# Moving the conditioning product from TensorE to VectorE, shortening a mixing round from ten J turns to eight, and loading exponential's table earlier

## The reference, cut to what matters

```python
b_c, c_c, h_c, q, k, v, g_conv, g_attn = split(xn @ w_in)
y_conv = b_c * causal_dwconv(c_c * h_c, conv_w_mix)
z = q @ k.T * scale                       # for each of 16 heads
log_fail = where(causal, log_sigmoid(z) - z, 0)
a = exp(log_sigmoid(z) + sums of log_fail over the keys between)
o = a @ v
merged = sigmoid(g_conv + b0) * (y_conv @ w_proj_conv) + sigmoid(g_attn + b1) * (o @ w_proj_attn)
mix = merged @ w_out
```

## Time and profile before

| | |
|---|---|
| time, median of 3 runs | 1852.38 us (1851.7 to 1852.97) |
| the profiled execution's own time | 1852.97 us |
| its span | 1851.2 us |
| PE busy | 1757.1 us (95%) |
| DVE, ACT, POOL busy | 1023.7, 897.6, 359.6 us |
| mixing stage (the eight rounds) | about 53 to 506 us of the span |
| gates; stage of `w_out` | about 506 to 678 us; 678 to 735 us |
| granted clock of PE, mean | 0.98 |
| a round in the middle of the mixing stage | 55.1 us |
| weights of a job (512 KB), median from issue to landing | 3.6 us |

### The profile page before, as it was taken

The page is one execution under the profiler, slowest core; times in us unless marked ns, Lnnn a source line. Parts: engine busy times, 40 slices in busy tenths (PEclk is TensorE's granted clock), DMA queues, the critical chain, the costliest instruction groups (busy, mean ns, idle before and its releaser), DMA issues.

```text
span 1851.2 us, 30779 instructions
## 1 busy us (share of the span) xinstructions
PE 1757.1 (95%) x11685; PEld 1574.6 (85%) x11685; DVE 1023.7 (55%) x1538; ACT 897.6 (48%) x1213; POOL 359.6 (19%) x520
## 2 busy tenths in 40 slices
PE   5899999999999999999999999999999999999996
PEld 5899999999999998899998888778877777788885
DVE  3455665655633336787565234477577777754443
ACT  3576666666633334333333222367565565633332
POOL 0011101111100003498880784000000000000001
PEclk9999999999999999799999997999999999999998
DMA  3222223222222235244333443665221221233332
GB/s 119 69 68 81 75 72 91 79 65 72 81 80 91 91 124 185 49 145 133 100 130 101 137 135 104 238 171 169 74 74 52 80 74 51 79 103 121 123 97 102
DMA packets 68034, 189.11 MB, mean 102 GB/s; under 512 B 15284, under 2 KB 19572, under 8 KB 67832
## 3 DMA queue, kind: packets, MB, share of 16 engines
q1 hardware_dynamic: 64040, 176.04, 30.2%
q0 software_dynamic: 3920, 12.06, 2.4%
HBM read 165.76 MB, written 19.95 MB: 100 GB/s over the span
## 4 chain that ended last, share of the span: by engine, by line
PE 70%; DVE 9%; ACT 9%; issue 6%; DMA 3%; POOL 1%; SPq 1%; ACTq 0%; DVEq 0%
PE J L870 25%; PE J L1139 17%; PE J L886 7%; PE J L1108 6%; DMA WR<-weights 3%; PE Z L926 2%; PE J L1274 2%; PE J L1264 2%; PE J L1319 2%; DVE WL L1874 2%; POOL E L2520 1%; DVE MX L2396 1%; ACT E L1477 1%; ACT E L1473 1%; PE Z L948 1%
## 5 line engine op out<-in xcount | busy, mean ns | idle before, releaser
L1874 DVE TENSOR_TENSOR WL<-WR,WH 128x1024 fp32r<-128x1024 f32 x271 | 356.3, 1316 | 310.8 <-ACT WH L1403 302.6
L1403 ACT ACTIVATE WH<-WR 128x1024 fp32r<-128x1024 f32 x271 | 285.3, 1054 | 241.7 <-DMA WR<-weights 118.6
L870 PE MATMUL J<-XH,WH 128*128 128x258 f32 (+1 forms) x1376 | 285.6, 289 | 30.8 <-issue 11.0
L870 PE MATMUL J<-XH,WL 128*128 128x258 f32 (+1 forms) x1376 | 281.8, 287 | 0.0
L870 PE MATMUL J<-XL,WH 128*128 128x258 f32 (+1 forms) x1376 | 275.7, 285 | 0.0
L870 PEld LDWEIGHTS J<-XH,WH 128*128 128x128 f32 x1376 | 219.6, 193 | 37.6 <-issue 26.3
L870 PEld LDWEIGHTS J<-XH,WL 128*128 128x128 f32 x1376 | 217.2, 193 | 0.0
L870 PEld LDWEIGHTS J<-XL,WH 128*128 128x128 f32 x1376 | 213.9, 191 | 0.1
L2520 POOL TENSOR_SCALAR_AFFINE_SELECT E<-E 128x128 f32<-128x128 f32 (+2 forms) x160 | 52.2, 364 | 449.3 <-DVE E L1953 239.1
L2538 POOL TENSOR_TENSOR SA<-SQ 128x512 f32<-128x512 f32 (+1 forms) x3 | 3.9, 1314 | 682.0 <-ACT SQ L1659 492.4
L1139 PE MATMUL J<-X2H,WH 128*128 128x512 f32 x168 | 68.8, 410 | 1.7 <-ACT X2H L1671 1.7
(11 more groups left out here) (432 smaller groups left out, 4162.9 us busy)
## 6 DMA issues: line engine op xcount, KB each, us to landing
WR<-weights SPq DMA_DIRECT2D x271, 512.0 KB, 3.6
CPS<-cp_dram SPq DMA_DIRECT2D x8, 576.0 KB, 6.0
cp_dram<-CQR POOLq DMA_DIRECT2D x16, 144.0 KB, 2.8
cp_dram<-CQI POOLq DMA_DIRECT2D x16, 144.0 KB, 2.8
X<-tokens SPq DMA_DIRECT2D x4, 528.0 KB, 5.3
H<-tokens SPq DMA_DIRECT2D x8, 264.0 KB, 3.8
bp_dram<-BQR POOLq DMA_DIRECT2D x8, 256.0 KB, 2.3
bp_dram<-BQI POOLq DMA_DIRECT2D x8, 256.0 KB, 3.1
```

Source lines behind the costliest of these rows:

```text
L870: mm = pe.matmul(o[:, 512 * h:512 * h + half], ws[:, s, w], xs[:, a:a + half], start=(k == 0 and i == 0 and part != WITH_LOW), stop=(k == ...
L1403: act.activation(WH[:, n % SPLIT, :], WR[:, n % RAW, :], ACT.Copy).then_inc(w_hi, 1)
L1874: dve.tensor_tensor(WL[:, n % SPLIT, :], WR[:, n % RAW, :], WH[:, n % SPLIT, :].bitcast(F32), ALU.subtract).then_inc(w_lo, 1)
```

## The change

The 24 `ada` jobs leave the stream of jobs. Their raw weights are loaded by SP into two buffers of their own, `AW`, three for each round of `gates`, and DVE multiplies them by the numbers of `c` and sums them (`modulation`), behind `ML` of each round of `gates`: two loads of four instructions of 256 columns and one of two instructions of 512 columns in a round, each waiting for the one before. In the stage of `w_out`, behind the second job, PE sums the partitions with 24 matmuls of one column (`sum_mod`), and DVE makes `MB` and `GG` behind the seventh. The way over DRAM, `turn_mod`, `CHL` and their copies go. ACT waits for the last `modulation` ahead of the first square of that stage.

The turned values go to `ZT` (four transposes) and a corner of job c_c's own `J` bank (`VTAIL`, one matmul), so that they take no turn; the empty turn goes as well. A round has eight turns, and job v now waits for the reading of q, no longer of k. PE waits for `v_lo` ahead of job b_c. A round has 6 weight jobs for 8. DVE does `head_out(h)` ahead of `YL`. Behind the logarithm of each `softplus` (and `head_out`), ACT runs an exponential of one column (`load_exp`). The loop's body holds two rounds for one, with the first two and the last two written out; DVE's `gates` is written out in full.

```diff
+            def load_ada(i):
+                if i >= 2:
+                    sp.wait_ge(ada_done, i - 1)
+                row = ROW_OUT + 2 * (i // 3) + 1 if i % 3 == 2 else ROW_MIX + 8 * (i // 3) + 6 + i % 3
+                sp.dma_start(AW[i % 2][:], weights[row]).then_inc(ada_landed[i % 2], 16)
+            for m in range(DT - 1):
+                load_weights(N_GATE + 4 * m + 4, ROW_GATE - N_GATE)
+                load_weights(N_GATE + 4 * m + 6, ROW_GATE - N_GATE)
+                if m == 0:
+                    sp.wait_ge(pv_done, HEADS)
+                for i in range(3 * m, 3 * m + 3):
+                    load_ada(i)
...
+            load_one(N_OUT)
+            load_one(N_OUT + 1)
+            for m in range(DT):
+                load_one(N_OUT + 2 + m)
                 if m == 0:
+                    for i in range(3 * DT - 3, 3 * DT):
+                        load_ada(i)
                     sp.wait_ge(job_done, N_OUT)
...
+            def sum_mod():
+                pe.wait_ge(ada_done, 3 * DT)
+                for b in range(24):
+                    src = MACC[:, P * b:P * (b + 1)] if b < 16 else MLAST[(b - 16) // 4][:, P * (b % 4):P * (b % 4 + 1)]
+                    mm = pe.matmul(ZT[:, b:b + 1], src, ONES[:, 0:1], start=b == 0, stop=True, skip_group_check=True)
+                mm.then_inc(mod_summed, 1)
...
             def turn_values(t):
-                pe.wait_ge(read_out[slot(t)], nth(t))
-                for kt in range(5):
-                    w = min(P, L1 - kt * P)
-                    mm = pe.transpose(J[t % 2][0:w, P * kt:P * (kt + 1)], VT[:, kt * P:kt * P + w], IDENT[:])
-                mm.then_inc(vt_done, 1)
+                for kt in range(4):
+                    pe.transpose(ZT[:, P * kt:P * (kt + 1)], VT[:, kt * P:(kt + 1) * P], IDENT[:])
+                pe.matmul(VTAIL[t % 2], VT[:, 4 * P:L1], IDENT[:],
+                          start=False, stop=True, skip_group_check=True).then_inc(vt_done, 1)
...
             def mix(m, last=False):                      # PE
-                n, t, h = N_MIX + 2 + 8 * m, T_MIX + 10 * m, 2 * m
-                job(n, t + 4, XH, XL)
+                n, t, h = N_MIX + 2 + 6 * m, T_MIX + 8 * m, 2 * m
+                job(n, t + 3, XH, XL)
                 pe.wait_ge(read_out[slot(t + 1)], nth(t + 1) + 1)
                 pe.wait_ge(read_out[slot(t + 2)], nth(t + 2) + 1)
                 scores(h)
                 if m.base or m.reg is not None:
-                    values(h - 1, t + 5)
-                job(n + 1, t + 6, XH, XL, start=LIVE, half=HALFK)
-                turn_values(t + 7)
-                ada(n + 2, 2 * P, True, False, m)
-                ada(n + 3, 2 * P, False, True, m)
-                job(n + 4, t + 8, XH, XL, start=LIVE, half=HALFK)
+                    values(h - 1, t + 4)
+                job(n + 1, t + 5, XH, XL, start=LIVE, half=HALFK)
+                turn_values(t + 5)
+                job(n + 2, t + 6, XH, XL, start=LIVE, half=HALFK)
                 accumulate(h)
-                job(n + 5, t + 9, XH, XL, start=LIVE, half=HALFK)
+                pe.wait_ge(v_lo, val(m + 1))
+                job(n + 3, t + 7, XH, XL, start=LIVE, half=HALFK)
                 scores(h + 1)
-                pe.wait_ge(read_out[slot(t + 7)], nth(t + 7) + 1)
-                values(h, t + 10)
...
+            def load_exp():                              # ACT
+                act.activation(EXP1[:], ONES[:, 0:1], ACT.Exp)
...
                 split_hi(n + 4)
                 softplus(h)
                 if later:
-                    head_out(h - 1, m - 1, t + 5)
+                    head_out(h - 1, m - 1, t + 4)
+                load_exp()
                 fail_hi(h)
...
-                split_hi(n + 6)
-                split_hi(n + 7)
-                split_hi(n + 8)
+                split_hi(n + 6)
                 weight_exp(h)
                 weight_hi(h)
-                split_hi(n + 9)
...
                 if not last:
-                    q_hi(m + 1, t + 11, n + 6)
-                    split_hi(n + 10)
-                    k_hi_(t + 12, n + 7)
+                    q_hi(m + 1, t + 9, n + 4)
+                split_hi(n + 7)
+                if not last:
+                    split_hi(n + 8)
+                    k_hi_(t + 10, n + 5)
...
+            def modulation(i):                           # DVE, three behind ML of each round of gates
+                raw, first, m = AW[i % 2], i % 3 == 0, i // 3
+                if i % 3 < 2:
+                    width, k0 = 2 * P, 4 * (i % 3)
+                    acc = MACC[:, 2 * P * m:2 * P * (m + 1)]
+                else:
+                    width, k0, first = 4 * P, 2 * (m % 4), m % 4 == 0
+                    acc = MLAST[m // 4][:]
+                count = JOB // width
+                dve.wait_ge(ada_landed[i % 2], 16 * (i // 2 + 1))
+                for k in range(count):
+                    w, c = raw[:, width * k:width * (k + 1)], CR[:, 2 * (k0 + k):2 * (k0 + k) + 1]
+                    if first and k == 0:
+                        ins = dve.tensor_scalar(acc, w, c, None, ALU.mult)
+                    else:
+                        ins = dve.scalar_tensor_tensor(out=acc, in0=w, scalar=c, in1=acc, op0=ALU.mult, op1=ALU.add)
...
             for m in range(DT):                          # ACT, stage of w_out
                 split_hi(n + 3)
-                split_hi(n + 4)
                 act.wait_ge(job_done, val(n + 1))
                 act.activation(halves(F[:, m * L1 + LIVE:(m + 1) * L1]), JK[t % 2], ACT.Copy)
+                if m == 0:
+                    act.wait_ge(ada_done, 3 * DT)
                 square(Q_MIX + m, JK[t % 2], HALFK)
```

More of the change, by code:

```diff
@@ L52 @@
 N_OUT2 = N_MERGE + 2 * DT
-ROW_ATT = N_ATT
+N_JOBS = N_OUT2 + DT
+ROW_MIX = 0
+ROW_GATE = ROW_MIX + 8 * DT
+ROW_OUT = ROW_GATE + 4 * DT
+ROW_UP = ROW_OUT + 2 * DT
+AFTER_UP = ROW_UP - N_UP
+ROW_ATT = N_ATT + AFTER_UP
 ROW_GLU = ROW_ATT + 2 * DT
 ROW_MERGE = ROW_GLU + 2 * DT
-N_LAST = N_OUT2 + DT
+N_LAST = N_JOBS + AFTER_UP
 RAW = 2
@@ L291, in build @@
         assert M3 + 160 + 2112 + 1600 <= 212800
-        MROW = sb("MROW", [P, 4 * P], M3 + 160)
+        MACC = sb("MACC", [P, 16 * P], M0)
+        MLAST = [sb("MLAST0", [P, 4 * P], M0 + 16 * P * 4), sb("MLAST1", [P, 4 * P], M3 + 160)]
+        assert 16 * P * 4 + 4 * P * 4 <= 4 * SCORE + 5120
+        AW = [sb(f"AW{x}", [P, JOB], M1 + 8480 + 4 * JOB * x) for x in range(2)]
+        assert M1 + 8480 + 8 * JOB <= M2
         assert M3 + 160 + 2048 <= 212800
@@ L461, in build @@
         JK = [halves(j[:])[:, :, 0:HALFK] for j in J]
+        VTAIL = [j[0:META, 384:512] for j in J]
         JO = [j[:, OUT_AT + LIVE:OUT_AT + L1] for j in J]
@@ L528, in build @@
         v_hi = sem("v_hi")
+        v_lo = sem("v_lo")
         conv_step = sem("conv_step")
@@ L546, in build @@
         mat_landed = sem("mat_landed")
[L547 to L550, removed]
+        ada_landed = [sem(f"ada_landed{x}") for x in range(2)]
+        ada_step = sem("ada_step")
+        ada_done = sem("ada_done")
+        mod_summed = sem("mod_summed")
+        mod_read = sem("mod_read")
         setup = sem("setup")
@@ L647, in load_weights @@
                         sp.wait_ge(w_lo, val(n + s - RAW + 1))
-                    sp.dma_start(WR[:, s, :], weights[cols(n + s, 1)].rearrange("a p n -> (a p) n"))\
+                    sp.dma_start(WR[:, s, :], weights[cols(n + s + shift, 1)].rearrange("a p n -> (a p) n"))\
                       .then_inc(w_landed[s], 16)
             def stream(first, last):
[L652 to L657, removed]
+                repeat(sp, (last - first) // RAW, 1, lambda i: load_weights(first + RAW * i, AFTER_UP))
             def load_row(n, row):
@@ L829, in _ @@
             repeat(sp, DT - 2, 2, lambda i: merge(i + 2))
-            for n in range(N_OUT2, N_LAST):
+            for n in range(N_OUT2, N_JOBS):
                 load_one(n)
@@ L1075, in _ @@
             for m in range(DT):
-                job(N_OUT + 2 * m, T_OUT + m, MH, ML, m_lo if m == 0 else None, start=LIVE, half=HALFK)
-                ada(N_OUT + 2 * m + 1, 4 * P, m % 4 == 0, m % 4 == 3, DT + m // 4)
+                job(N_OUT + m, T_OUT + m, MH, ML, m_lo if m == 0 else None, start=LIVE, half=HALFK)
+                if m == 1:
+                    sum_mod()
             last_squares(Q_MIX + DT - 1, HALFK)
@@ L1115, in _ @@
                     if m == 1:
-                        turn_mod()
                         pe.wait_ge(r_ready, 3)
@@ L1421, in _ @@
             act.wait_ge(in_landed, 32)
-            act.activation(CHL[:].rearrange("p k x -> p (k x)"), CR[:], ACT.Copy).then_inc(w_hi, 1)
             for m in range(DT):
@@ L1515, in mix @@
                     weight_hi(h - 1)
-                src = job_result(t + 4, n)
+                src = job_result(t + 3, n)
                 if positive(m):
                     act.wait_ge(vt_done, val(m))
```

(12 more changed lines are left out.)

156 lines of the change are left out of this document (67 added, 89 removed).

## The result

After, the median is 1807.61 us (1806.41 to 1808.87, four runs), against 1852.04 in the runs of before beside it: a ratio of 0.9765, with a 95% interval of 0.9752 to 0.9777. The forecast was 1803, with a range of 1793 to 1819. The profiled execution took 1806.46 us, 46.5 less than the one of before, where the sum said 49.3.

A forecast was written before the change was run, and what follows sets the result against it. The prediction took PE's own work, plus 3 us a round of waits set by a chain over ACT, POOL and DVE, as the bound. 16.8 + 22.0 + 5.1 - 0.8 + 5.9 + 0.3 = 49.3 us gave 1803, range 1793 to 1819.

The forecast's parts named there:

- Ada jobs in mixing and waits, 38.8: Mixing stage: PE saves 16.8 us of ada matmuls over eight rounds and 22.0 us of its waits.
- the two terms, 16.8 and 22.0: Mixing stage: 2.1 us of ada matmuls in each of eight rounds, and 22.0 of 25.3 us of PE waits, would go.
- Waits that stay, 3.3: Mixing stage: of PE's 25.3 us of waits, 0.9, 1.9 and 0.5 would remain.
- The 1.9 for the empty turn: First round: job h_c would wait 1.9 us for the empty turn, given by DVE behind its sum `E`.
- the 0.5 for loads at the head of the loop: Rounds 2, 4 and 6: a table load ahead of `weight_exp(h-1)` makes PE wait 0.2 us, 0.5 in all.
- The clock, 5.1: Mixing stage: two late low-clock stretches go, giving back 5.1 us; alternatives were 1808 (chance 0.12) and 1800 (0.08).
- the 8.5 of the upper bound: Mixing stage: 8.5 us given back if all four low-clock stretches go.
- Gates, 0: Gates: DVE's block ends at T + 11.3 with 4.8 us of cover, so PE loses 0.
- Stage of `w_out`, 5.9: Stage of `w_out`: 7.4 for ada jobs plus 2.5 of waiting, less 3.0 and 1.0: 5.9 us gained, from 3 to 7.
- I take 3.0: Stage of `w_out`: the 24 added one-column matmuls cost 2.0 to 3.8 us, taken as 3.0.
- The 0.8 for DVE's turn: Stage of `w_out`: the first square, held for DVE's turn behind the sums and a conversion, costs 0.8 us, up to 3.
- Early table load: Mixing stage: if a load stays ahead of `weight_exp` everywhere, 3 us are lost, giving 1806; chance 0.04.

The follow-up runs named there:

- few ada: Kernel before with 2 of the 16 ada matmuls left in each mixing round: 1849.59 us, ratio 0.9996 to before.
- both waits: Kernel after, with PE waiting for k's result to be read ahead of job v and for `CT` ahead of job h_c: 1852.2 us, ratio 1.0009 to before.
- the last-round experiment: Kernel after, with ACT's exponential table load and `weight_exp` ahead of the second conversion in the first round of gates: 1803.68 us, ratio 0.9748 to before.
- the wait for `CT` alone: Kernel after, with PE waiting ahead of job h_c until ACT has copied c_c's result: 1830.13 us, ratio 0.9892 to before.
- the wait for k alone: Kernel after, with PE's waits for the reading of q and k moved ahead of job v: 1823.44 us, ratio 0.9859 to before.
- Threefold: Kernel after with each conditioning instruction of DVE done three times: 1862.66 us, ratio 1.0059 to before.
- twofold: Kernel after with each conditioning instruction of DVE done twice: 1817.13 us, ratio 0.9825 to before.

## Why the prediction was right, and where its terms were off

**Ada jobs in mixing and waits, 38.8.** Right, as a sum. The next stage's first job starts 44.1 us earlier (510.80, now 466.73), against 43.1 by the forecast's terms up to there. By the rows of both traces it is 16.8 (as read before the change), 21.5 of waits (25.3 less 3.8), 6.8 for the clock (8.5 less 0.30 of the last 5.7 us) and 0.8 off for `VTAIL`, 44.3. But the two terms, 16.8 and 22.0, are not two gains. The ada work alone gives nothing (few ada); its removal with both waits left in gives nothing either (both waits). The prediction's first paragraph said that work counts only if the chain gets shorter, yet what it worked out for that were `AL`, `OL` and `KL`; for `CT` it had 0.22 in round 4 and then "Job h_c now starts where the ada jobs did", without asking what ends the wait. With the ada jobs gone this was the largest wait of all, 1.9 a round; the values' own bank, which the prediction gave no price, removes it and is worth 22.5. The bank is the one that the ada jobs wrote to, so the parts could not have been had singly in this form.

**Waits that stay, 3.3.** Measured 3.8 (0.8 and 3.0), in other places. Job v's 0.8 is the 0.9 forecast. The 1.9 for the empty turn did not come, nor the 0.5 for loads at the head of the loop, where the trace has none: its exponential loads are those of `load_exp`, one for each head, and one each in the first and the last round. The 3.0 for `AL` in the last round was not foreseen: it comes from a late load of weights ahead of the exponential on ACT, and the last-round experiment took 1.9 of it away.

**The clock, 5.1.** All four low stretches of the mixing stage went, as its clock of 1.00 says, which is the 8.5 of the upper bound; a new one stands behind the wait for `AL` (0.76 over 14 us, 3.4 lost). The difference, 5.1, is that of the forecast by chance, and half of the new loss falls in gates. By the Trainium skill ("TensorE: Matmul & The Clock Gate", Part 1) the gate follows how busy TensorE has lately been; the runs agree. Of the seven windows of 50 us from 103 to 453 us, 0.97 stands in five with both waits, in one with the wait for `CT` alone, and in none with the wait for k alone or in after; the others have 1.00. A low first pair stands behind the waits of 2.5 and 3.7 us shown.

**Gates, 0.** DVE's block was shorter than forecast (0.52 from start to start for 256 columns, not 0.64, as the gap of 0.16 that the forecast put between dependent instructions does not stand in this code; T + 10.0 for T + 11.3) and the cover is 6.1, not 4.8. Threefold and twofold bracket where it ends. Gates took 169.0 for 167.3, 1.6 more, from the low clock at its start.

**Stage of `w_out`, 5.9.** Measured 3.0, the largest miss. The step that failed is "I take 3.0" for `sum_mod`, and it is a misreading of the earlier trace rows: `x12` there counts 12 records of six matmuls (516 tokens in six blocks of 86), two records for each. The 24 matmuls are 48 records, so the same rows give 4.0 to 7.7, and the 5.34 measured lies between. A further 1.6 went to the job behind it, whose clock is low (0.54 from 652.6 to 656). The 0.8 for DVE's turn was hidden under the sums, and is a wait of 2.53 when they are spread.

**Early table load.** The forecast put a load that stays ahead of `weight_exp` at 3 us in the new kernel. The runs say at most 1 there, as the load falls into idle time of ACT; 6 is its worth in the old order, by its trace most of it in the clock. The Trainium skill ("ScalarE: Activation LUTs", What ACT_TABLE_LOAD costs) has 2.66 us for a switch, about 1283 ns for the load and the rest for a drain. The trace agrees on the load, 1.28 each, but the next activation starts 1.29 behind its start; no drain shows, and the measurement decides.

**Between executions.** The stages give 44.1 - 1.6 + 3.0 = 45.5, and the other 1.0 of the 46.5 lies later (0.3 was forecast for `turn_mod`). The sum was for the profiled execution: 1803.7 forecast, 1806.46 measured. The medians differ by 44.4 rather than 46.5; about 2 us of difference is spread between executions, of no cause that these runs separate. Not tried: the old order of turns without the ada jobs and with conversions left in, which would price the conversions by themselves.

## What to carry to other kernels

Work on the bounding engine can be cover for a chain beside it. Before taking it away, find the wait that stands right behind it, however small (here 0.22 in round 4), and work out how large it becomes; remove both, or neither. Work moved to an idle engine is free up to a cover that can be read as the time from its start to the first consumer of what is queued behind it; doing it twice and three times on the chip showed that edge within a few us.

## What the runs showed of the hardware that was not expected

- In the first round job h_c did not wait for the empty turn: it started at 69.41, when DVE's sum had hardly begun:

```profile
69.32 1.56 DVE L1949 SCALAR_TENSOR_TENSOR E<-Z,E 128x1348 f32<-128x1348 f32 x1 [5.53 <-ACT E L1470]
```

  The empty instruction queued behind the sum set the turn free at about the sum's start, not its end. It was so in the kernel before as well: the sum started at 73.84, and the transposes that waited for the empty instruction at 73.93. The forecast's 1.9 took the sum's end.
- A matmul of one column in f32 is two records of about 0.11 us, 48 records in 5.34 us. At a clock of 0.64 and then 0.50 the same 48 took 9.0.
- The 0.16 between dependent DVE instructions goes with the loop, not with their width. In after, the same two instructions of 516 columns (0.76 each) stand 0.15 apart in a round that the loop holds (228.14), and follow each other in 1.55 for both in the rounds that are written out, here the first:

```profile
79.15 1.55 DVE L2039 SCALAR_TENSOR_TENSOR CV<-PP,PRM,CV 128x516 f32<-128x516 f32 x2
```

  DVE's `gates` is written out too, and seven of 256 columns took 3.61 us there, each waiting for the one before.
- In the twofold run a wait of 3.4 us cost 7.1, as the work behind it ran at the lower clock.
